# Differential attention on one core: GpSimd combines the two attention maps by itself, and the transposes follow two steps behind

## The chip, the cores and the metric

The kernel runs on one core of a Trainium2 chip. The metric is the device time of one execution in microseconds (us), as the median of several runs.

## The reference, cut to what matters

One layer of a hybrid backbone works on 2048 sample tokens and 128 prompt tokens. It normalises and projects them, runs a differential attention beside a short gated convolution, and projects the result. The change touches the attention of the sample tokens alone:

```python
s = einsum('bqhmd,bkhmd->bhmqk', qblk, k) * scale     # m = 0, 1: two maps per head
p = softmax(s, axis=-1)
a = p[:, :, 0] - lam * p[:, :, 1]                     # the combine
out = einsum('bhqk,bkhe->bqhe', a, v)
```

There are 4 heads, 2048 queries and 2176 keys (2048 samples and 128 cached ones), head dimension 64 and value dimension 128. All is float32.

## The kernel before, in words

The kernel has five stages: modulation, projections, convolution, attention (about 935 us to 1718 us of the profiled execution) and the output projection. Each engine has a program of its own, written out by hand; engines meet only at semaphores (`wait_ge`), and each engine takes its instructions in order.

**Attention** goes in 64 steps (NT), one for each head and tile of 128 queries. Step n works on the scores of tile n and on later stages of earlier tiles. It has four parts, p = 0 to 3. In each part TensorE (PE) computes 128x1024 scores of one map and one half of the keys (L761), VectorE (DVE) takes their maximum (L1380), and ScalarE (ACT) writes their exponentials to `e0` (map 0, four buffers) or `e1` (map 1, two buffers) with the sums beside them (L1070). The 128 cached keys are a small third piece (`PIECES`: 0 to 1024, 1024 to 2048, 2048 to 2176). Scores alternate between two pairs of PSUM banks, so part p waits for the exponentials of part p - 2.

Each piece has a maximum of its own. So small operations bring the pieces to one scale: DVE L1402 and L1405 at the end of step n, an exponential on ACT (L1082), then in part 0 of step n + 1 DVE L1388, L1394 and L1398 (the reciprocal of the softmax sum). GpSimd (POOL) waits for L1398 and makes six factors per row from it (L596, L598): one for each map and piece, with 1 or -lambda in it.

**The combine** of tile n, before the change, is divided. GpSimd multiplies all three pieces of `e1` by their factors (L603, with the factor broadcast as a second tensor), then the middle piece of `e0` (L606), and adds the two middle pieces (L610). VectorE does the first and the third piece in one pass each (`combine`, L1362: `e0` times factor plus `e1`), two steps behind the scores (S_COMB = 2), in part 0 and part 2.

**Behind it**, three steps behind (S_TR = 3), PE transposes the 17 blocks of the combined map (L742, groups of 4, 4, 4, 4 and 1). ACT copies the groups 0, 1, 2 and 4 out of PSUM (L1023), and DVE copies group 3 (`tr_dve`, L1355). Group 3 shares its bank with group 1 of the next tile, so PE waits for that copy (L738). Five steps behind (S_PV = 5), the product with v is made for two tiles at once, a half of the keys in each step (L750), and ACT takes it out (L1031) and stores it (S_OUT = 7).

The order of DVE's work in part 0 is: maximum, combine of piece 0, L1388, `tr_dve`, L1394, L1398. SP loads q for each step, k once per head, and v in two halves when the products of the last head have released them.

After step 63 come drain steps. In them DVE also splits blocks of `w_out` (`wo_lo`, L1347) and does the softmax of the prompt (`prompt_maps`). ACT waits for blocks of `w_out`, and SP loads the next ones when DVE has released their buffer. The output stage begins with a PE operation at L819.

Of the kernel before, what the change touches and what calls it, by code (L numbers as in the profile page):

```python
# [61 lines left out]
S_COMB, S_TR, S_PV, S_OUT = 2, 3, 5, 7  # L62
# [12 lines left out]
def hymba_layer(nc, a):  # L75
# [8 lines left out]
    with ctx:  # L84
# [25 lines left out]
        tick = sb("tick", [P, 1])  # L110
        cw = sb("cw", [P, 4])
# [199 lines left out]
        def _(sp):  # L311
# [157 lines left out]
            for it in range(ITS):  # L469
                head = it // 4  # L470
                for t in range(4):
                    sp.wait_ge(s_pair, 4 * (4 * it + t + 1))
                    if it == 4 * (H - 1) and t == 0:
                        load_wo(0)
                        load_wo(1)
                    if it % 4 == 0 and t == 0 and head + 1 < H:
                        load_k(head + 1)
                    if it % 4 == 0 and head > 0 and t == 3:
                        sp.wait_ge(pv_mm, 4 * it - 1)
                        load_v(head, 0)  # L480
                    if it % 4 == 1 and head > 0 and t == 0:
                        sp.wait_ge(pv_mm, 4 * (it - 1))
                        load_v(head, 1)
                    if it + 1 < ITS:
                        load_q(t, (it + 1) // 4, ((it + 1) % 4) * 4 * P + t * P)
# [60 lines left out]
        def _(pool):  # L546
# [73 lines left out]
        def _(pe):  # L620
# [109 lines left out]
            def transposes(n, t, g):  # L730

                j0, cnt = TGROUPS[g]
                if g == 0:
                    pe.wait_ge(a_ready, 2 * (n + 1))
                    pe.wait_ge(a1_ready, n + 1)

                if g == 1:
                    wait(pe, t_dve, n)  # L738
                else:
                    wait(pe, t_act, {0: 4 * n - 1, 2: 4 * n + 1, 3: 4 * n + 2, 4: 4 * n}[g])  # L740
                for i in range(cnt):
                    mm = pe.transpose(trbank(g)[:, i * P:(i + 1) * P], e0[:, t, (j0 + i) * P:(j0 + i + 1) * P], ident)  # L742
                mm.then_inc(t_mm, 1)
# [20 lines left out]
            def step(it, t, sc=True, tr=True, tr_last=True, pv=True):  # L764
                n = 4 * it + t
                for p in range(4):
# [12 lines left out]
                    if pv:  # L779
                        half = 1 - t % 2  # L780
                        b = 0 if t in (1, 2) else 1
                        if p == 1 - half:
                            pe.wait_ge(s_v[half], (32 if half else 16) * ((it + (2 if t == 0 else 3)) // 4))
                            if half == 0:
                                pe.wait_ge(t_act, 4 * (n - 4) + 3)
                                wait(pe, att_evac, 2 * it - (2 if t == 1 else 1))
                            else:
                                pe.wait_ge(t_act, 4 * (n - 4))
                                pe.wait_ge(t_dve, n - 4)
                        product(b, half, p)  # L790
# [17 lines left out]
            for n in range(NT, NT + S_PV):  # L808
                step(n // 4, n % 4, sc=False, tr=n < NT + S_TR, tr_last=n <= NT + S_TR)
                if n == NT + 2:  # L810
                    prompt_transposes()
                if n == NT + 4:
                    prompt_product()
# [41 lines left out]
        def _(act):  # L855
# [170 lines left out]
            def att_out(it, t):  # L1026

                pb = 1 if t == 1 else 0
                act.wait_ge(pv_mm, 4 * it + t - S_PV)
                wait(act, att_stored[pb], 16 * (it - (2 if t == 1 else 1)))  # L1030
                act.activation(atto[:, pb], ps[:, 7, pb * 2 * P:(pb + 1) * 2 * P], ACT.Copy).then_inc(att_evac, 1)  # L1031

            def att_store(it, t):

                pb = 1 if t == 1 else 0
                act.wait_ge(att_evac, 2 * it - (2 if t == 1 else 1))
                u = it - (2 if t == 1 else 1)
# [7 lines left out]
            def step(it, t, sc=True, tr=True, tr_last=True, out=True):  # L1045
                n = 4 * it + t
                b = t % 2
                for p in range(4):
# [3 lines left out]
                    if sc and p == 3:  # L1052
                        act.wait_ge(mxc_done, n + 1)
                        wait(act, a_ready, 2 * (n - 1))
# [6 lines left out]
                    if sc:  # L1061
# [3 lines left out]
                        if p == 2:  # L1065
                            wait(act, a_ready, 2 * (n - 1) - 1)
                        if p == 3:
                            wait(act, a1_ready, n - 1)
# [15 lines left out]
            for it in range(3):  # L1084
                for t in range(4):
                    n = 4 * it + t
                    step(it, t, tr=n >= S_TR, tr_last=n > S_TR, out=n >= S_OUT and t % 2 == 1)
            with act.Fori(3, ITS) as it:
                for t in range(4):
                    step(it, t, out=t % 2 == 1)  # L1090
            for n in range(NT, NT + S_OUT - 1):
                step(n // 4, n % 4, sc=False, tr=n < NT + S_TR, tr_last=n <= NT + S_TR,
                     out=n % 2 == 1)
# [4 lines left out]
                if n == NT + 2:  # L1098
                    act.wait_ge(a_ready, 2 * NT)
# [46 lines left out]
        def _(dve):  # L1146
# [224 lines left out]
            def step(it, t, sc=True, den=True, comb=True, tr_last=True):  # L1371
                n = 4 * it + t
                b = t % 2
                for p in range(4):
# [9 lines left out]
                    if p == 0 and comb:  # L1384
                        combine(n - S_COMB, (t - S_COMB) % 4, 0)
# [4 lines left out]
                    if p == 0 and tr_last:  # L1390
                        tr_dve(n - 1 - S_TR, (t - 1 - S_TR) % 4)
# [15 lines left out]
                    if p == 2 and comb:  # L1407
                        combine(n - S_COMB, (t - S_COMB) % 4, 2)
# [5 lines left out]
            for it in range(2):  # L1414
                for t in range(4):
                    n = 4 * it + t
                    step(it, t, den=n >= 1, comb=n >= S_COMB, tr_last=n > S_TR)
# [3 lines left out]
            for n in range(NT, NT + S_TR + 1):  # L1421
                step(n // 4, n % 4, sc=False, den=n == NT, comb=n < NT + S_COMB, tr_last=n <= NT + S_TR)
# [136 lines left out]
```

## Time and profile before

| | us |
|---|---|
| median of 3 runs | 1938.04 (1937.11 to 1943.31) |
| the profiled execution | 1940.76 |
| its span in the profile | 1939.0 |
| PE busy (8596 instructions) | 1763.6 (91%) |
| DVE busy (1500) | 1173.9 (61%) |
| POOL busy (614) | 749.1 (39%) |
| ACT busy (1505) | 720.2 (37%) |
| mean granted TensorE clock | 0.971 of full speed |

A row of the timeline gives the start, the duration, the engine, the line, the operation and what it writes and reads; in square brackets stands how long the engine was idle before it and what released it. Rows of one line that follow each other closely are merged (x3). Times are us, in groups also ns where marked. PE's ends are modelled. PEld is the loading of PE's weights.

### The profile page before, as it was taken

What the parts mean: (1) busy time and instruction counts of PE and PEld (TensorE: products, weight loads), DVE (VectorE), ACT (ScalarE), POOL (GpSimd) and SP (SyncE); (2) the same over time, 40 slices, a digit from 0 to 9 for tenths busy, and PEclk for the clock granted to TensorE, in tenths of its full rate; (3) what the DMA queues carried; (4) which work ended last, traced back from release to release, by engine and by line L of the source; (5) the groups of instructions that cost most, each with busy time, mean ns of one, the idle gap of its engine ahead of it and who ended that gap; (6) DMA issues with size and microseconds to landing.
All of it is one profiled execution on the core that took longest, in us unless ns stands there. A gap on an engine that the chain in (4) does not pass through costs nothing.

```text
span 1939.0 us, 25390 instructions
## 1 busy us (share of the span) xinstructions
PE 1763.6 (91%) x8596; PEld 1488.4 (77%) x8596; DVE 1173.9 (61%) x1500; ACT 720.2 (37%) x1505; POOL 749.1 (39%) x614
## 2 busy tenths in 40 slices
PE   7799999989999999998589999889999999659999
PEld 2478888878999989998367777767777777548889
DVE  0554588872232332423688888888888888655553
ACT  2443233331010100100466666666666666431110
POOL 0000488880000000000477777777777777400000
PEclk9899999999999999999799999999999999879999
DMA  9233222331020110101710031113001100146441
GB/s 352 95 109 104 80 99 91 105 117 52 29 90 19 41 68 28 68 19 45 186 35 29 27 85 39 31 47 79 27 27 51 53 27 16 46 170 241 176 141 48
DMA packets 121890, 154.79 MB, mean 80 GB/s; under 512 B 10224, under 2 KB 111344, under 8 KB 120688
## 3 DMA queue, kind: packets, MB, share of 16 engines
q1 hardware_dynamic: 116704, 149.69, 24.0%
q10 hardware_dynamic: 5136, 4.46, 0.7%
q8 instruction: 28, 0.46, 0.1%
q14 instruction: 22, 0.18, 0.0%
HBM read 104.04 MB, written 50.07 MB: 79 GB/s over the span
## 4 chain that ended last, share of the span: by engine, by line
PE 68%; DVE 16%; issue 6%; DMA 4%; ACT 3%; SPq 2%; POOL 0%; DVEq 0%; ACTq 0%; POOLq 0%
PE ps L634 34%; PE ps L836 10%; PE ps L761 8%; DVE e L1362 8%; PE ps L750 7%; PE ps L742 4%; PE ps L626 3%; DVE stt L1380 2%; ACT scr L919 2%; PE ps L651 2%; DVE at L1355 1%; DMA wad<-in_w_ada 1%; PE ps L819 1%; DMA worw<-in_w_out 1%; ACT scr L881 1%
## 5 line engine op out<-in xcount | busy, mean ns | idle before, releaser
L634 PE MATMUL ps<-hT,w 128*128 128x448 f32 (+1 forms) x3360 | 694.1, 366 | 12.6 <-DVE w L1169 12.6
L634 PEld LDWEIGHTS ps<-hT,w 128*128 128x128 f32 x3360 | 623.9, 189 | 76.2 <-issue 27.1
L761 PE MATMUL ps<-kb,qb 128*128 (+1 forms) x1280 | 340.0, 397 | 47.9 <-ACT e L1070 30.8
L1070 ACT ACTIVATE e<-ps,stt 128x1024 f32<-128x1024 f32 x256 | 285.7, 1116 | 259.3 <-DVE stt L1380 235.7
L1380 DVE TENSOR_REDUCE stt<-ps 128x1 f32<-128x1024 f32 x256 | 312.2, 1220 | 97.3 <-PE ps L761 96.9
L750 PE MATMUL ps<-at,vb 128*128 128x256 f32 x1088 | 281.2, 390 | 9.2 <-ACT atto L1031 9.2
L761 PEld LDWEIGHTS ps<-kb,qb 128*128 128x128 f32 x1280 | 208.1, 194 | 84.3 <-ACT e L1070 39.3
L596 POOL TENSOR_TENSOR stt<-stt,lamc 128x2 f32<-128x2 f32 x64 | 12.6, 197 | 660.9 <-DVE stt L1398 660.9
L603 POOL TENSOR_TENSOR e<-e,stt 128x1024 f32<-128x1024 f32 (+1 forms) x192 | 262.8, 1397 | 5.0
L750 PEld LDWEIGHTS ps<-at,vb 128*128 128x128 f32 x1088 | 211.1, 197 | 48.4 <-issue 9.7
L742 PE MATMUL ps<-cst,e 128*128 128x128 f32 x1088 | 175.7, 280 | 57.6 <-DVE at L1355 56.6
L1362 DVE SCALAR_TENSOR_TENSOR e<-e,stt 128x1024 f32<-128x1024 f32 (+1 forms) x128 | 225.6, 1762 | 0.0
L742 PEld LDWEIGHTS ps<-cst,e 128*128 128x128 f32 x1088 | 131.0, 142 | 112.0 <-DVE at L1355 82.1
L836 PE MATMUL ps<-mix,wo 128*128 128x448 f32 (+1 forms) x960 | 205.1, 373 | 7.2 <-DVE mix L1455 7.2
L836 PEld LDWEIGHTS ps<-mix,wo 128*128 128x128 f32 x960 | 181.7, 192 | 27.5 <-DVE mix L1455 7.6
L610 POOL TENSOR_TENSOR e<-e 128x1024 f32<-128x1024 f32 x64 | 152.5, 2383 | 9.2
L985 ACT ACTIVATE scr<-ps 128x448 f32<-128x448 f32 (+1 forms) x40 | 20.9, 533 | 352.7 <-PE ps L634 352.7
L1217 DVE RECIPROCAL qx<-qx 128x448 f32<-128x448 f32 (+1 forms) x40 | 114.8, 2870 | 49.8 <-ACT qx L950 49.7
L565 POOL TENSOR_TENSOR qx<-qx,scr 128x448 f32<-128x448 f32 (+1 forms) x40 | 45.8, 1146 | 241.3 <-DVE qx L1221 238.9
L1023 ACT ACTIVATE at<-ps 128x512 f32<-128x512 f32 (+1 forms) x256 | 124.3, 511 | 23.1 <-PE ps L742 22.8
L606 POOL TENSOR_TENSOR e<-e,stt 128x1024 f32<-128x1024 f32 x64 | 125.2, 1956 | 0.0
L634 PE MATMUL ps<-w,hT 128*128 128x512 f32 x408 | 98.1, 401 | 7.3 <-DVE hT L1201 7.3
(108 smaller groups left out, 1374.4 us busy)
## 6 DMA issues: line engine op xcount, KB each, us to landing
raw<-in_w_in SPq DMA_DIRECT2D x32, 512.0 KB, 3.8
qb<-spill_q SPq DMA_DIRECT2D x256, 64.0 KB, 2.3
wad<-in_w_ada SPq DMA_DIRECT2D x6, 2048.0 KB, 9.0
scr<-in_xT SPq DMA_DIRECT2D x8, 1024.0 KB, 5.7
kb<-spill_k SPq DMA_DIRECT2D x8, 1024.0 KB, 9.7
spill_k<-scr SPq DMA_DIRECT2D x32, 224.0 KB, 2.1
spill_q<-scr SPq DMA_DIRECT2D x32, 224.0 KB, 2.2
spill_cv<-scr SPq DMA_DIRECT2D x32, 224.0 KB, 2.2
```

The costliest lines, as they stand in the source:

```text
L603: pool.tensor_tensor(e1[:, b, k0:k1], e1[:, b, k0:k1], stt[:, b, 7, 3 + c:4 + c].to_broadcast([P, k1 - k0]), ALU.mult)\
L606: pool.tensor_tensor(e0[:, t, k0:k1], e0[:, t, k0:k1], stt[:, b, 7, 1:2].to_broadcast([P, k1 - k0]), ALU.mult)\
L610: pool.tensor_tensor(e0[:, t, k0:k1], e0[:, t, k0:k1], e1[:, b, k0:k1], ALU.add).then_inc(a1_ready, 1)
L634: mm = pe.matmul(out, slot_of(l, j), rhs_of(r, j), start=(i == 0 and j == 0), stop=(i == 2 and j == DJ - 1))
L742: mm = pe.transpose(trbank(g)[:, i * P:(i + 1) * P], e0[:, t, (j0 + i) * P:(j0 + i + 1) * P], ident)
L750: mm = pe.matmul(ps[:, 7, b * 2 * P:(b + 1) * 2 * P], vb[:, js[i]], at[:, b, 0, js[i], :], start=(half == 0 and i == 0), stop=(half == 1 a ...
L761: mm = pe.matmul(out[:, c0 - k0:c1 - k0], qb[:, t, ver, m], keys, start=(ver == 0), stop=(ver == 1))
L836: mm = pe.matmul(ps[:, k % 4, 0:n], wo[:, o, l, j], mix[:, tg % 2, r, j, 0:n], start=(half == 0 and i == 0 and j == H), stop=(half == 1 an ...
L1023: act.activation(at[:, t // 2, 0, j0:j0 + cnt, (t % 2) * P:(t % 2 + 1) * P], trbank(g).rearrange("p (j q) -> p j q", j=cnt), ACT.Copy).the ...
L1070: act.activation(dst[:, c * 1024:(c + 1) * 1024], ps[:, 2 * c:2 * c + 2, :].rearrange("p c n -> p (c n)"), ACT.Exp, bias=stt[:, b, 0, 3 * ...
L1362: dve.scalar_tensor_tensor(e0[:, t, k0:k1], e0[:, t, k0:k1], stt[:, t % 2, 7, c:c + 1], e1[:, t % 2, k0:k1], ALU.mult, ALU.add).then_inc(a ...
L1380: dve.tensor_reduce(stt[:, b, 0, 3 * m + c:3 * m + c + 1], ps[:, 2 * c:2 * c + 2, :].rearrange("p c n -> p (c n)"), AX.X, ALU.max, negate= ...
```

## The change

GpSimd multiplies both maps, piece by piece, with `tensor_scalar` and the factor as a per-partition scalar. It does so in two parts: the first 1024 keys with their own sum (and the semaphore `a_ready`), then the other 1152 keys (`a1_ready`). One small operation (into a new tile `gate`) stands before the first multiplication. VectorE does nothing of the combine, and copies group 3 before L1388. Transposes, products and stores each come one step earlier; group 0 waits for the first part, group 2 for the second. The halves of the product, the loads of v and the waits are renumbered to match.

```diff
-S_COMB, S_TR, S_PV, S_OUT = 2, 3, 5, 7
+S_TR, S_PV, S_OUT = 2, 4, 6
...
-                    if it % 4 == 0 and head > 0 and t == 3:
+                    if it % 4 == 0 and head > 0 and t == 2:
                         sp.wait_ge(pv_mm, 4 * it - 1)
                         load_v(head, 0)
-                    if it % 4 == 1 and head > 0 and t == 0:
-                        sp.wait_ge(pv_mm, 4 * (it - 1))
+                    if it % 4 == 0 and head > 0 and t == 3:
+                        sp.wait_ge(pv_mm, 4 * it)
                         load_v(head, 1)
...
+            def pieces(n, t, which):
+                b = t % 2
+                for c in which:
+                    k0, k1 = PIECES[c]
+                    pool.tensor_scalar(e1[:, b, k0:k1], e1[:, b, k0:k1], stt[:, b, 7, 3 + c:4 + c], None, ALU.mult)\
+                        .then_inc(e1_done, 1)
+                    pool.tensor_scalar(e0[:, t, k0:k1], e0[:, t, k0:k1], stt[:, b, 7, c:c + 1], None, ALU.mult)\
+                        .then_inc(e0_done, 1)
...
                 pool.wait_ge(coef_done, n + 1)
-                for c in (0, 2, 1):
-                    k0, k1 = PIECES[c]
-                    pool.tensor_tensor(e1[:, b, k0:k1], e1[:, b, k0:k1],
-                                       stt[:, b, 7, 3 + c:4 + c].to_broadcast([P, k1 - k0]), ALU.mult)\
-                        .then_inc(e1_done, 1)
-                pool.tensor_tensor(e0[:, t, k0:k1], e0[:, t, k0:k1], stt[:, b, 7, 1:2].to_broadcast([P, k1 - k0]), ALU.mult)\
-                    .then_inc(e0_done, 1)
+                pool.tensor_tensor(gate[:], lamc[:], lamc[:], ALU.mult)
+                pieces(n, t, (0,))
+                pool.wait_ge(e1_done, 3 * n + 1)
+                pool.wait_ge(e0_done, 3 * n + 1)
+                pool.tensor_tensor(e0[:, t, 0:1024], e0[:, t, 0:1024], e1[:, b, 0:1024], ALU.add).then_inc(a_ready, 1)
+                pieces(n, t, (1, 2))
                 pool.wait_ge(e1_done, 3 * (n + 1))
-                pool.wait_ge(e0_done, n + 1)
-                pool.tensor_tensor(e0[:, t, k0:k1], e0[:, t, k0:k1], e1[:, b, k0:k1], ALU.add).then_inc(a1_ready, 1)
+                pool.wait_ge(e0_done, 3 * (n + 1))
+                pool.tensor_tensor(e0[:, t, 1024:KEYS], e0[:, t, 1024:KEYS], e1[:, b, 1024:KEYS], ALU.add)\
+                    .then_inc(a1_ready, 1)
...
                 if g == 0:
-                    pe.wait_ge(a_ready, 2 * (n + 1))
+                    pe.wait_ge(a_ready, n + 1)
+                if g == 2:
                     pe.wait_ge(a1_ready, n + 1)
...
-            def combine(n, t, c):
-
-                k0, k1 = PIECES[c]
-                dve.wait_ge(e1_done, 3 * n + (1 if c == 0 else 2))
-                dve.scalar_tensor_tensor(e0[:, t, k0:k1], e0[:, t, k0:k1], stt[:, t % 2, 7, c:c + 1],
-                                         e1[:, t % 2, k0:k1], ALU.mult, ALU.add).then_inc(a_ready, 1)
...
-                    if p == 0 and comb:
-                        combine(n - S_COMB, (t - S_COMB) % 4, 0)
+                    if p == 0 and tr_last:
+                        tr_dve(n - 1 - S_TR, (t - 1 - S_TR) % 4)
                     if p == 0 and den:
                         dve.wait_ge(f_done, n)
                         dve.tensor_tensor(stt[:, 1 - b, 4, :], stt[:, 1 - b, 3, :], stt[:, 1 - b, 1, :], ALU.mult)\
                             .then_inc(fz_done, 1)
-                    if p == 0 and tr_last:
-                        tr_dve(n - 1 - S_TR, (t - 1 - S_TR) % 4)
...
-                    if p == 2 and comb:
-                        combine(n - S_COMB, (t - S_COMB) % 4, 2)
```

## Rows read from the trace of the kernel before

**Rows 1.** Busy by stretch: length; PE, PEld, DVE, ACT, POOL; clock, DMA.
```profile
1240.00:1560.00 320.00, 287.73 (x1509) 233.64 (x1510) 273.24 (x365) 208.43 (x487) 244.91 (x196) 0.98 0.16 46
```

**Rows 2.** Who waited for whom, 1000 to 1560 us: total us, times, longest.
```profile
POOL stt L596 <- DVE stt L1398: 119.0, 48, 4.1
...
PEld ps L742 <- DVE at L1355: 60.4, 48, 2.1
```

**Rows 3.** Chain that ended last, 1240 to 1300 us: start us, us, what.
```profile
1260.59 2.25 DVE e L1362
...
1262.91 0.61 DVE at L1355
...
1263.57 0.66 PE ps L742 x4
```

**Rows 4.** Timeline of POOL: one step; first and last L596 of 64.
```profile
941.95 0.20 POOL L596 TENSOR_TENSOR stt<-stt,lamc 128x2 f32<-128x2 f32 x1 [508.41 <-DVE stt L1398]
...
1263.86 0.20 POOL L596 TENSOR_TENSOR stt<-stt,lamc 128x2 f32<-128x2 f32 x1 [2.10 <-DVE stt L1398]
...
1264.42 4.10 POOL L603 TENSOR_TENSOR e<-e,stt 128x1024 f32<-128x1024 f32 x3
1268.48 1.94 POOL L606 TENSOR_TENSOR e<-e,stt 128x1024 f32<-128x1024 f32 x1
1270.57 2.38 POOL L610 TENSOR_TENSOR e<-e 128x1024 f32<-128x1024 f32 x1
...
1666.30 0.23 POOL L596 TENSOR_TENSOR stt<-stt,lamc 128x2 f32<-128x2 f32 x1 [2.10 <-DVE stt L1398]
```

**Rows 5.** Busy by stretch: two neighbouring steps (columns of rows 1).
```profile
1263.86:1275.28 11.42, 11.42 (x64) 9.56 (x63) 9.29 (x14) 7.35 (x17) 8.79 (x8) 1.00 0.08 23
1275.28:1286.45 11.17, 8.79 (x50) 6.92 (x49) 10.28 (x14) 7.63 (x18) 8.77 (x8) 1.00 0.11 35
```

**Rows 6.** Groups by form on POOL: busy us, mean ns of one.
```profile
L603 POOL TENSOR_TENSOR e<-e,stt 128x1024 f32<-128x1024 f32 x128 | 242.5, 1895 | 5.0
L610 POOL TENSOR_TENSOR e<-e 128x1024 f32<-128x1024 f32 x64 | 152.5, 2383 | 9.2
L606 POOL TENSOR_TENSOR e<-e,stt 128x1024 f32<-128x1024 f32 x64 | 125.2, 1956 | 0.0
...
L603 POOL TENSOR_TENSOR e<-e,stt 128x128 f32<-128x128 f32 x64 | 25.7, 402 | 0.0
```

**Rows 7.** Groups by form on ACT and DVE: busy us, mean ns of one.
```profile
L1070 ACT ACTIVATE e<-ps,stt 128x1024 f32<-128x1024 f32 x256 | 285.7, 1116 | 259.3 <-DVE stt L1380 235.7 <-PE ps L742 23.3
...
L1362 DVE SCALAR_TENSOR_TENSOR e<-e,stt 128x1024 f32<-128x1024 f32 x64 | 116.2, 1815 | 0.0
L1362 DVE SCALAR_TENSOR_TENSOR e<-e,stt 128x128 f32<-128x128 f32 x64 | 109.4, 1709 | 0.0
...
L1057 ACT ACTIVATE e<-ps,stt 128x128 f32<-128x128 f32 x128 | 45.9, 364 | 18.9 <-DVE stt L1411 18.9
```

**Rows 8.** Timeline around one held DVE operation, about 1317 us.
```profile
1315.84 2.37 POOL L610 TENSOR_TENSOR e<-e 128x1024 f32<-128x1024 f32 x1
...
1317.17 1.05 DVE L1405 TENSOR_TENSOR stt<-stt 128x6 f32<-128x6 f32 x1
```

**Rows 9.** Timeline of DVE: L1388 before the L596 of rows 4.
```profile
1262.76 0.15 DVE L1388 TENSOR_TENSOR stt<-stt 128x6 f32<-128x6 f32 x1
```

**Rows 10.** Busy by stretch: a lower clock (columns of rows 1).
```profile
1309.00:1323.00 14.00, 14.00 (x70) 11.68 (x70) 10.55 (x15) 7.47 (x17) 9.44 (x10) 0.88 0.52 118
```

**Rows 11.** Timeline of the drain, 1683 to 1718 us.
```profile
1683.17 0.68 DVE L1355 COPY at<-ps 128x512 f32<-128x512 f32 x1
...
1691.33 0.69 DVE L1355 COPY at<-ps 128x512 f32<-128x512 f32 x1 [7.22 <-PE ps L742]
...
1696.93 2.36 DVE L1347 TENSOR_TENSOR wo<-worw,wo 128x1024 fp32r<-128x1024 f32 x2 [4.90 <-ACT wo L1015]
...
1718.19 1.86 PE L819 MATMUL ps<-csq,cst 128*128 128x448 f32 x2 [11.47 <-ACT csq L1118]
```

More of the change, by code:

```diff
@@ L110, in hymba_layer @@
         tick = sb("tick", [P, 1])
+        gate = sb("gate", [P, 2])
         cw = sb("cw", [P, 4])
@@ L779, in step @@
                     if pv:
-                        half = 1 - t % 2
-                        b = 0 if t in (1, 2) else 1
+                        half = t % 2
+                        b = t // 2
                         if p == 1 - half:
-                            pe.wait_ge(s_v[half], (32 if half else 16) * ((it + (2 if t == 0 else 3)) // 4))
+                            pe.wait_ge(s_v[half], (32 if half else 16) * ((it + 3) // 4))
                             if half == 0:
-                                pe.wait_ge(t_act, 4 * (n - 4) + 3)
-                                wait(pe, att_evac, 2 * it - (2 if t == 1 else 1))
-                            else:
-                                pe.wait_ge(t_act, 4 * (n - 4))
-                                pe.wait_ge(t_dve, n - 4)
+                                pe.wait_ge(t_act, 4 * (n - 3) + 3)
+                                wait(pe, att_evac, 2 * it - (2 if t == 0 else 1))
+                            else:
+                                pe.wait_ge(t_act, 4 * (n - 3))
+                                pe.wait_ge(t_dve, n - 3)
                         product(b, half, p)
@@ L811, in _ @@
                     prompt_transposes()
-                if n == NT + 4:
+                if n == NT + 3:
                     prompt_product()
@@ L1026, in att_out @@
             def att_out(it, t):
-                pb = 1 if t == 1 else 0
+                pb = 1 if t == 0 else 0
                 act.wait_ge(pv_mm, 4 * it + t - S_PV)
-                wait(act, att_stored[pb], 16 * (it - (2 if t == 1 else 1)))
+                wait(act, att_stored[pb], 16 * (it - (2 if t == 0 else 1)))
                 act.activation(atto[:, pb], ps[:, 7, pb * 2 * P:(pb + 1) * 2 * P], ACT.Copy).then_inc(att_evac, 1)
             def att_store(it, t):
-                pb = 1 if t == 1 else 0
-                act.wait_ge(att_evac, 2 * it - (2 if t == 1 else 1))
-                u = it - (2 if t == 1 else 1)
+                pb = 1 if t == 0 else 0
+                act.wait_ge(att_evac, 2 * it - (2 if t == 0 else 1))
+                u = it - (2 if t == 0 else 1)
                 q0 = (u % 4) * (4 * P) + pb * 2 * P
@@ L1053, in step @@
                         act.wait_ge(mxc_done, n + 1)
-                        wait(act, a_ready, 2 * (n - 1))
+                        wait(act, a1_ready, n - 1)
                         for mc in range(2):
@@ L1065, in step @@
                         if p == 2:
-                            wait(act, a_ready, 2 * (n - 1) - 1)
-                        if p == 3:
-                            wait(act, a1_ready, n - 1)
+                            wait(act, a_ready, n - 1)
                         dst = e0[:, t] if m == 0 else e1[:, b]
@@ L1086, in _ @@
                     n = 4 * it + t
-                    step(it, t, tr=n >= S_TR, tr_last=n > S_TR, out=n >= S_OUT and t % 2 == 1)
+                    step(it, t, tr=n >= S_TR, tr_last=n > S_TR, out=n >= S_OUT and t % 2 == 0)
             with act.Fori(3, ITS) as it:
                 for t in range(4):
-                    step(it, t, out=t % 2 == 1)
+                    step(it, t, out=t % 2 == 0)
             for n in range(NT, NT + S_OUT - 1):
                 step(n // 4, n % 4, sc=False, tr=n < NT + S_TR, tr_last=n <= NT + S_TR,
-                     out=n % 2 == 1)
+                     out=n % 2 == 0)
                 if n == NT:
@@ L1098, in _ @@
                 if n == NT + 2:
-                    act.wait_ge(a_ready, 2 * NT)
+                    act.wait_ge(a_ready, NT)
                     act.wait_ge(a1_ready, NT)
@@ L1369, in three, with step @@
                 return x.rearrange("p (m c) -> p m c", m=2)
-            def step(it, t, sc=True, den=True, comb=True, tr_last=True):
+            def step(it, t, sc=True, den=True, tr_last=True):
                 n = 4 * it + t
@@ L1416, in _ @@
                     n = 4 * it + t
-                    step(it, t, den=n >= 1, comb=n >= S_COMB, tr_last=n > S_TR)
+                    step(it, t, den=n >= 1, tr_last=n > S_TR)
             with dve.Fori(2, ITS) as it:
@@ L1420, in _ @@
                     step(it, t)
-            for n in range(NT, NT + S_TR + 1):
-                step(n // 4, n % 4, sc=False, den=n == NT, comb=n < NT + S_COMB, tr_last=n <= NT + S_TR)
+            for n in range(NT, NT + S_TR + 2):
+                step(n // 4, n % 4, sc=False, den=n == NT, tr_last=n <= NT + S_TR)
                 if n == NT:
```

## The prediction

> **What bounds the kernel now.** I first read the busy time by stretch, to find the stage that matters and how full each engine is in it. In the attention PE is busy 287.7 of 320 us, DVE 273.2, POOL 244.9 and ACT 208.4 [rows 1]. No engine is full, so the next view is who waits for whom. PE waits for DVE's copy of group 3 (60.4 us in 48 waits of its weight loads), and POOL waits for DVE's reciprocal, 119.0 us in 48 waits [rows 2]. The chain of waits says why: the combine L1362 (2.25 us) stands before the copy, and the transposes start at once behind the copy [rows 3]. So DVE, in order and with 3.5 us of combine in each step (1.815 + 1.709 us), sets the pace [rows 7]. Of that 3.5 us a large part is standing still: the piece of 128 columns takes 1709 ns, almost as long as the one of 1024.
>
> The first L596 is at 941.95 and the last of 64 at 1666.30 [rows 4]. That is 724.35 us for 63 steps, 11.5 us for one. Two neighbouring steps take 11.42 and 11.17 us; PE is busy 11.42 and 8.79 of them, 20.2 us in two [rows 5]. So PE alone would allow 10.1 us a step, and POOL needs 9.1 us from L596 to the end of L610 (1263.86 to 1272.95) [rows 4].
>
> **DVE's part.** 3.5 us a step go. The 320 us of [rows 1] hold 28 steps, with 9.8 us of DVE in each; 6.3 are left. DVE then has room, and the copy of group 3 comes right behind the first maximum. PE's wait for it goes. What is late next is POOL.
>
> **POOL's step, added up.** Now it has six multiplications and two sums. The sums have a row: 2.38 us for 1024 columns [rows 4]; for 1152 columns 2.65 us, with (2383 - 189) / 1024 = 2.14 ns for each column more [rows 6]. The multiplication with a per-partition scalar has none on POOL. Its bounds come from two rows. From above, the multiplication by a broadcast tensor: 1895 ns for 1024 columns and 402 for 128, so 1.67 ns a column and 189 ns fixed [rows 6]. From below, an engine that reads one tensor and takes a per-partition operand: ACT's exponentials take 1116 ns for 1024 columns and 364 for 128, so 0.84 ns a column [rows 7]. The first is 1.99 times the second, as if POOL spent one slot of 0.84 ns on each operand that it reads, even on one number read again and again. With one operand read, one slot is left: 189 + 1024 x 0.84 = 1.05 us, and 0.30 us for 128 columns. I take that, because the operands are ACT's kind and the fixed part is POOL's. The ends are 0.9 us (ACT's slot, hardly any fixed part) and 1.9 us.
>
> Consecutive POOL instructions start 0.04 us before the last one's end (4.10 us for three that last 4.19), and a sum waits 0.15 us behind the product that it needs [rows 4]. The step then runs: L596 at 0, the small operation into the gate tile at 0.56 (where the first product is now), the first product at 0.72, the second at 1.73, the sum at 2.93. The other four products start at 5.26, 6.27, 7.28 and 7.54, the second sum at 7.99, and it ends at 10.64. That is 10.6 us, more than PE's 10.1: POOL becomes the bound. To it I add 0.1 for two DVE operations that slip in between (L606, with a held one behind it, takes 1956 ns against 1895 [rows 6]) and 0.2 for reading six scalars, a guess whose ends are 0 and 0.6. **10.9 us a step.**
>
> Because POOL is the bound from its first tile on (steps 0 and 1 have no transposes), it needs no wait for DVE: 63 x 10.9 = 686.7 us against 724.35, **37.7 us less**. Now and then a step takes about 1.9 us more while the granted clock is lower, 0.88 in such a stretch [rows 10]. POOL's backlog covers these; if that cover were gone, seven of them would give back 13 us.
>
> **Waits.** Group 0 wants the first part, ready 5.3 us after L596, and group 2 the second, at 10.7. PE reaches group 2 of tile n half way through step n + 2, some 14 us behind L596 of tile n. So a POOL step of up to 11 us is in time, and what PE waits is POOL's pace, not latency. ACT's third part of step n waits for the first part of tile n - 2, which is long done. The four buffers of `e0` suffice, since the transposes come earlier too. SP's loads of v move one step up with the products that release and need them; the distance is the same, and the load of q behind them is wanted a whole round later. I cost these at nothing; a load of v that came late would be seen once per head. The small operation is counted above (0.16 us).
>
> **The drain.** From the last L596 to the first L819 it is 51.9 us (1666.30 to 1718.19) [rows 4, 11]. Behind the prompt's softmax DVE copies a group 3 at 1683.17 and the next at 1691.33, and only at 1696.93 come the third and fourth block of w_out, on which loads and the output stage hang [rows 11]. With S_TR = 2 one tile fewer is open there: 1683.17 to 1691.33, **8.2 us less**. The ends are 0 (the loads of w_out set it anyway) and 13.8 (1683.17 to 1696.93, all of it).
>
> **Sum.** -37.7 - 8.2 = -45.9 us: the profiled execution's 1940.8 (span 1939.0 and 1.8 around it) becomes 1894.9. The median of the runs is 2.7 us below that execution, so 1892 us. A difference under 0.3% (6 us) can't be told from none.
>
> **Rivals.**
> *A. POOL's product stays slow.* One operand less does not help, because the loop over columns sets the time. At the broadcast row's 1.9 us the step is 10.9 + 4 x 0.84 + 2 x 0.1 = 14.5 us, so 63 x 14.5 = 913 us, and 1938 + 189 - 8 = 2119 us. It is slower from (724.35 + 8.2) / 63 = 11.6 us a step, a product of 1.22 us. For it: every large POOL row here is at 1.67 ns a column or above. Against it: the factor of 1.99. I give 0.12 to about 1.9 us and 0.11 to values between 1.25 and 1.7 us (1941 to 2062 us). The Trainium skill, GPSIMD Engine Reference, section on elementwise work, gives about 1.8 cycles an element as the best case of a tight loop; an estimate from that is 1.7 us a product and 13.6 us a step, which is in this case. The same page calls one-input work roughly line rate, which is in mine; no row here decides between them.
>
> *B. DVE and POOL lock each other out (slower).* A DVE operation of six columns, L1405, takes 1.05 us at 1317.17 and ends when POOL's sum ends (1315.84 + 2.37 = 1318.21) [rows 8]. L1388 is of the same kind, and it starts 1.1 us before the L596 that depends on it [rows 4, 9]. Before, POOL is always idle at that moment. Now it is in its last sum for 2.65 us. If L1388 arrives there, it is held to the end, and 1.1 us pass before POOL goes on: 10.8 + 1.1 = 11.9 us a step, 750 us, 1938 + 25 - 8 = 1955 us. It decides if L1388 comes later than 8.0 us into POOL's step. Against it: POOL starts with a backlog, as steps 0 and 1 are short, and PE's own wait for group 2 places L1388 at about 7.3 us. That is close; a step at the lower clock may tip it. Chance 0.12. The Trainium skill, SBUF — State Buffer, "Who interferes with whom", says that a VectorE instruction with two SBUF inputs and a reading GpSimd instruction exclude each other for a whole instruction; by that rule the trace agrees, with the 1.05 us above.
>
> *C. POOL is faster than I take it.* At 0.9 us a product and no time for scalars the step is 10.1 us, where PE is the bound: 636 us, 1938 - 88 - 8 = 1842 us at best, 1867 with half way to it. Chance 0.07.
>
> *D. About nothing.* A product of 1.2 us and 11.6 us a step: chance 0.06.
>
> **How the numbers follow.** My case (products of 1.0 to 1.15 us) has 0.52: 1875 to 1920 us. The range from 1866 to 1968 takes in this, D, B and about half of C and the near end of A's middle values; it leaves out the slow product and most of its middle. Faster is my case, C and a little of D: 0.60. Same is the rest of D: 0.05. Slower is A and B: 0.35.
>
> **What the profile after would show.** POOL busy for over 9 of 11 us, with hardly any idle time before L596; a product of about 1.05 us for 1024 columns; 63 steps in about 687 us. No combine on DVE, no wait of PE for L1355, instead one for POOL at group 2. L1388 and L1405 at times held for up to 2.6 us. What would make me wrong: a product over 1.22 us, or idle time of 1.1 us before L596 in each step while L1388 lasts over 1 us (rival B), or PE full again.

## The result, and the profile after

The changed kernel takes 2367.09 us (median of 4 runs, 2364.85 to 2370.27), the kernel before 1937.57 beside it: a ratio of 1.221, with a 95% interval from 1.218 to 1.224. It is slower by 430 us. The prediction was 1892 us, with a range up to 1968; even its slowest rival ended at 2119.

GpSimd's groups by form in the changed kernel (busy us, mean ns of one; the rows of before are [rows 6]):

```profile
L601 POOL TENSOR_SCALAR e<-e,stt 128x1024 f32<-128x1024 f32 x128 | 365.4, 2855 | 0.0
L599 POOL TENSOR_SCALAR e<-e,stt 128x1024 f32<-128x1024 f32 x128 | 364.3, 2846 | 0.1
L620 POOL TENSOR_TENSOR e<-e 128x1152 f32<-128x1152 f32 x64 | 167.0, 2609 | 9.5
L616 POOL TENSOR_TENSOR e<-e 128x1024 f32<-128x1024 f32 x64 | 150.1, 2346 | 9.5
...
L601 POOL TENSOR_SCALAR e<-e,stt 128x128 f32<-128x128 f32 x64 | 38.7, 605 | 0.0
L599 POOL TENSOR_SCALAR e<-e,stt 128x128 f32<-128x128 f32 x64 | 38.7, 604 | 0.0
```

The product with a per-partition scalar takes 2.85 us for 1024 columns and 0.60 for 128. I had put it at 1.05 and 0.30, with 1.9 as the upper end for 1024. The two sums are as computed (2.35 and 2.61 us against 2.38 and 2.65). One step of GpSimd, with the start of the next, and the first and last of the 64 (timeline; [rows 4] before):

```profile
939.11 0.20 POOL L607 TENSOR_TENSOR stt<-stt,lamc 128x2 f32<-128x2 f32 x1 [503.80 <-DVE stt L1399]
...
1509.94 0.20 POOL L607 TENSOR_TENSOR stt<-stt,lamc 128x2 f32<-128x2 f32 x1
1510.21 0.20 POOL L609 TENSOR_TENSOR stt<-stt 128x6 f32<-128x6 f32 x1
1510.49 0.20 POOL L612 TENSOR_TENSOR gate<-lamc 128x2 f32<-128x2 f32 x1
1510.66 2.85 POOL L599 TENSOR_SCALAR e<-e,stt 128x1024 f32<-128x1024 f32 x1
1513.49 2.85 POOL L601 TENSOR_SCALAR e<-e,stt 128x1024 f32<-128x1024 f32 x1
1516.48 2.37 POOL L616 TENSOR_TENSOR e<-e 128x1024 f32<-128x1024 f32 x1
...
1525.81 2.61 POOL L620 TENSOR_TENSOR e<-e 128x1152 f32<-128x1152 f32 x1
1528.37 0.20 POOL L607 TENSOR_TENSOR stt<-stt,lamc 128x2 f32<-128x2 f32 x1
...
2099.11 0.20 POOL L607 TENSOR_TENSOR stt<-stt,lamc 128x2 f32<-128x2 f32 x1
```

Only the first L607 has idle time before it: from then on GpSimd never waits for VectorE, and a step is what its instructions add up to, 18.4 us (1509.94 to 1528.37). The 63 steps take 1160.0 us against 724.35, so +435.7. The drain, from the last L607 to the first operation of the output stage (2145.89), is 46.8 us against 51.9, so -5.1; the first combine starts 2.8 us earlier. That sums to +427.8 us, beside 426.5 by the spans (2365.5 and 1939.0).

The same stretch as [rows 1] (columns as there), and the waits in 1000 to 1560 us (us in total, times, longest; [rows 2] before):

```profile
1240.00:1560.00 320.00, 218.20 (x951) 174.75 (x950) 132.24 (x193) 132.62 (x304) 312.15 (x191) 0.85 0.11 30
```

```profile
DVE stt L1383 <- PE ps L773: 321.1, 122, 7.0
...
PE ps L754 <- POOL e L620: 99.4, 30, 4.4
...
PE ps L754 <- POOL e L616: 77.6, 30, 5.0
```

GpSimd is busy for 312 of 320 us; PE fell from 288 to 218, and waits for both sums (L616, L620). No wait for DVE's copy is left. The granted clock is 0.85 in this stretch, against 0.98. PE's idle time goes before the low clock in these rows (busy by stretch, columns of [rows 1]):

```profile
1506.20:1510.10 3.90, 0.00 (x0) 0.00 (x0) 0.00 (x0) 0.78 (x2) 3.75 (x4) 0.89 0.00 0
1510.10:1511.20 1.10, 1.09 (x5) 1.10 (x6) 0.00 (x0) 0.00 (x0) 0.94 (x4) 0.50 0.00 0
...
1516.30:1518.90 2.60, 2.31 (x13) 1.63 (x11) 1.23 (x2) 0.00 (x0) 2.45 (x3) 1.00 1.02 202
```

PE does nothing for 3.9 us, then works at 0.50, the lower of its two levels (1.2 of 2.4 GHz), where four transposes take 1.11 us, and later at 1.00, where they take 0.60. The same comes again a step later, at 1528.50 us. Since GpSimd's chain has no gaps, the low clock costs the steps nothing.

### The profile page after: what moved, and what is told of

It reads as the page before. It is cut to its first block, busy times and chain, and to the rows that moved or that the text cites. A ratio compares the mean times of both kernels' runs of the same rounds, so it can differ in the third digit from the quotient of the medians.

```text
span 2365.5 us, 25394 instructions
## 1 busy us (share of the span) xinstructions
PE 1899.8 (80%) x8596; PEld 1595.3 (67%) x8596; DVE 1033.2 (44%) x1372; ACT 727.2 (31%) x1505; POOL 1336.1 (56%) x870
## 4 chain that ended last, share of the span: by engine, by line
POOL 42%; PE 40%; issue 9%; DMA 3%; DVE 3%; ACT 2%; SPq 0%; POOLq 0%; ACTq 0%; DVEq 0%
PE ps L645 28%; POOL e L601 17%; POOL e L599 17%; PE ps L848 8%; POOL e L620 5%; PE ps L637 2%; ACT scr L931 1%; PE ps L662 1%; DMA wad<-in_w_ada 1%; POOL e L616 1%; PE ps L831 1%; DMA worw<-in_w_out 1%; POOL stt L609 1%; POOL gate L612 1%; DMA raw<-in_w_in 1%
## 5 line engine op out<-in xcount | busy, mean ns | idle before, releaser
L754 PE MATMUL ps<-cst,e 128*128 128x128 f32 x1088 | 220.9, 330 | 381.3 <-POOL e L620 213.1
L754 PEld LDWEIGHTS ps<-cst,e 128*128 128x128 f32 x1088 | 159.5, 170 | 457.4 <-issue 160.2
L773 PE MATMUL ps<-kb,qb 128*128 (+1 forms) x1280 | 406.6, 457 | 20.0 <-DMA kb<-spill_k 16.1
L601 POOL TENSOR_SCALAR e<-e,stt 128x1024 f32<-128x1024 f32 (+1 forms) x192 | 404.1, 2105 | 0.0
L599 POOL TENSOR_SCALAR e<-e,stt 128x1024 f32<-128x1024 f32 (+1 forms) x192 | 403.0, 2099 | 0.1
L762 PE MATMUL ps<-at,vb 128*128 128x256 f32 x1088 | 328.8, 440 | 0.0
L607 POOL TENSOR_TENSOR stt<-stt,lamc 128x2 f32<-128x2 f32 x64 | 12.6, 197 | 503.8 <-DVE stt L1399 503.8
L773 PEld LDWEIGHTS ps<-kb,qb 128*128 128x128 f32 x1280 | 251.5, 232 | 54.5 <-issue 19.1
L762 PEld LDWEIGHTS ps<-at,vb 128*128 128x128 f32 x1088 | 246.6, 230 | 53.6
L1035 ACT ACTIVATE at<-ps 128x512 f32<-128x512 f32 (+1 forms) x256 | 130.9, 513 | 289.6 <-PE ps L754 289.5
L620 POOL TENSOR_TENSOR e<-e 128x1152 f32<-128x1152 f32 x64 | 167.0, 2609 | 9.5
L616 POOL TENSOR_TENSOR e<-e 128x1024 f32<-128x1024 f32 x64 | 150.1, 2346 | 9.5
```

The lines of the kernel that those rows point to most:

```text
L599: pool.tensor_scalar(e1[:, b, k0:k1], e1[:, b, k0:k1], stt[:, b, 7, 3 + c:4 + c], None, ALU.mult)\
L601: pool.tensor_scalar(e0[:, t, k0:k1], e0[:, t, k0:k1], stt[:, b, 7, c:c + 1], None, ALU.mult)\
L616: pool.tensor_tensor(e0[:, t, 0:1024], e0[:, t, 0:1024], e1[:, b, 0:1024], ALU.add).then_inc(a_ready, 1)
L620: pool.tensor_tensor(e0[:, t, 1024:KEYS], e0[:, t, 1024:KEYS], e1[:, b, 1024:KEYS], ALU.add)\
L762: mm = pe.matmul(ps[:, 7, b * 2 * P:(b + 1) * 2 * P], vb[:, js[i]], at[:, b, 0, js[i], :], start=(half == 0 and i == 0), stop=(half == 1 a ...
L773: mm = pe.matmul(out[:, c0 - k0:c1 - k0], qb[:, t, ver, m], keys, start=(ver == 0), stop=(ver == 1))
```

## The experiments

Theory 1 was that GpSimd is the only bound and that the price of its single-operation product, above what the broadcast product costs, explains the time. Its rival, theory 2, was that the new structure (two parts, two steps behind, small VectorE operations among long GpSimd ones) costs something by itself. Each ratio is to the kernel before, run beside it on the same chip; its median was 1940.6 to 1941.1 us.

**1. The broadcast product back**

```diff
-pool.tensor_scalar(e1[:, b, k0:k1], e1[:, b, k0:k1], stt[:, b, 7, 3 + c:4 + c], None, ALU.mult)
+pool.tensor_tensor(e1[:, b, k0:k1], e1[:, b, k0:k1],
+                   stt[:, b, 7, 3 + c:4 + c].to_broadcast([P, k1 - k0]), ALU.mult)   # and e0 likewise
```

> The changed kernel, but GpSimd multiplies with tensor_tensor and the factor broadcast, as the kernel before did; all else as changed. Theory 1 (GpSimd is the only bound, and its product with a per-partition scalar, 2.85 us for 1024 columns and 0.60 for 128, is the whole loss): a step is 18.4 us less 4 x 0.97 and 2 x 0.22, so 14.1 us, and the run takes 2367 - 63 x 4.3 = 2095 us. Theory 2 (the two-part structure or the distance of two steps costs something by itself, by waits and held VectorE operations): it stays above 2150 us, with idle time on GpSimd.

Measured: 2095.7 us, ratio 1.080 (1.078 to 1.081). Steps run from 942.92 to 1830.63, so 14.09 us each, with no idle time before L609 (L607 of the changed kernel) but before the first. Theory 1 holds to a microsecond; 271 of the 430 us are the choice of this instruction. The other 155 us or so are what the moved work costs even at the broadcast product's 1.90 us, where PE would allow 10.1 us a step. The structure itself costs nothing that shows at this pace.

**2. A price list.** Ahead of the first combine, GpSimd does single operations on spare tiles, each waited for:

```diff
+for i in range(3): done(pool.tensor_scalar(v[:, 0:1024], v[:, 0:1024], s, None, ALU.mult))              # L639
+for i in range(3): done(pool.tensor_scalar(v[:, 0:512], v[:, 0:512], s, None, ALU.mult))                # L641
+for i in range(3): done(pool.tensor_scalar(v[:, 0:1024], v[:, 0:1024], 0.5, None, ALU.mult))            # L643
+...
+for i in range(3): done(pool.tensor_scalar(v[:, 0:1024], v[:, 0:1024], s, 0.5, ALU.mult, ALU.add))      # L647
+for i in range(3): done(pool.tensor_copy(v[:, 0:1024], w_[:, 0:1024]))                                  # L649
+...
```

> The changed kernel, with 29 GpSimd operations more ahead of the first combine, one after the other, on spare tiles: products with a per-partition scalar, with a constant, with a scalar and a second constant, copies, products with a broadcast and with a full tensor. Theory 1a (reading the scalar through a pointer is what costs): with a constant the product of 1024 columns takes about 1.05 us, and with a pointer 2.85. Theory 1b (the loop of this operation costs it, whatever the scalar is): both take 2.85 us, and the copy, which reads one tensor too, says whether one read is cheap at all (1.05 us) or not. The total says nothing; it is that of the changed kernel and some 50 us.

The whole run, one execution, took 2416.5 us; its rows by form (mean ns of one) are what counts:

```profile
L639 POOL TENSOR_SCALAR vpad<-vpad,sublns 128x1024 f32<-128x1024 f32 x3 | 8.5, 2848 | 0.3
L643 POOL TENSOR_SCALAR vpad<-vpad 128x1024 f32<-128x1024 f32 x3 | 8.3, 2770 | 0.3
...
L653 POOL TENSOR_TENSOR vpad<-vpad,sublns 128x1024 f32<-128x1024 f32 x3 | 5.7, 1893 | 0.2
L641 POOL TENSOR_SCALAR vpad<-vpad,sublns 128x512 f32<-128x512 f32 x3 | 4.7, 1564 | 0.3
L647 POOL TENSOR_SCALAR vpad<-vpad,sublns 128x1024 f32<-128x1024 f32 x3 | 3.4, 1122 | 0.3
L649 POOL COPY vpad<-ppad 128x1024 f32<-128x1024 f32 x3 | 3.1, 1040 | 0.2
...
L651 POOL COPY vpad<-ppad 128x128 f32<-128x128 f32 x3 | 0.9, 296 | 0.2
```

The pointer is not to blame: with a constant the product still takes 2.77 us, so theory 1a falls. One more column costs this form (2848 - 1564) / 512 = 2.51 ns, and the copy (1040 - 296) / 896 = 0.83 ns. But the same instruction with a second operation (times the scalar, plus a constant) takes 1.12 us, hardly more than a copy. Neither theory had that.

**3. Products as short as the prediction took them to be.** They run over 306 and 6 columns; the kernel leaves the other columns without their factor.

```diff
+cut = k0 + (306 if c < 2 else 6)
-pool.tensor_scalar(e1[:, b, k0:k1], e1[:, b, k0:k1], stt[:, b, 7, 3 + c:4 + c], None, ALU.mult)
+pool.tensor_scalar(e1[:, b, k0:cut], e1[:, b, k0:cut], stt[:, b, 7, 3 + c:4 + c], None, ALU.mult)   # and e0 likewise
```

> The changed kernel with products over 306 of each 1024 columns and 6 of 128, so that each takes the 1.05 and 0.30 us that the prediction had assumed (the other columns are left without their factor). Theory 1 (only the price of the product was wrong): a step takes 10.6 to 10.9 us, 63 steps 668 to 687 us, and the run 1875 to 1900 us, as predicted for that price (1892). Theory 2 (VectorE's small operations and GpSimd lock each other out, or the new structure waits): 11.9 us a step and 1955 us or more, with 1.1 us of idle time before each L607.

Measured: 1884.9 us, ratio 0.971 (0.969 to 0.972). The products take 1.07 us, 63 steps run from 941.40 to 1621.83, so 10.80 us each, and the drain is 42.5 us. At the price that I had assumed, the total of the prediction (1892 us) was right to 0.4%, and its parts, 10.9 and 43.7 us, to 1% and 3%. The lockout of rival B does happen in small: L1407, six columns wide, takes 1.7 us on average.

```profile
L1407 DVE TENSOR_TENSOR stt<-stt 128x6 f32<-128x6 f32 x64 | 110.1, 1721 | 2.2
...
L1392 DVE TENSOR_TENSOR stt<-stt 128x6 f32<-128x6 f32 x64 | 14.7, 229 | 0.0
```

But it is L1407 (L1405 before) that is held, at the end of a step, and hardly L1392 (L1388 before), on which GpSimd waits: 0.23 us against 0.15. So the loop does not close.

**4. VectorE's order alone, in the kernel before**

```diff
-if p == 0 and comb: combine(n - S_COMB, (t - S_COMB) % 4, 0)
+if p == 0 and tr_last: tr_dve(...)            # now directly behind the maximum
 ...                                           # L1388
-if p == 0 and tr_last: tr_dve(...)
 ...                                           # L1394 and L1398, now L1392 and L1396
+if p == 0 and comb: combine(n - S_COMB, (t - S_COMB) % 4, 0)
```

> The kernel before, with one thing moved in VectorE's part 0: the copy of group 3 directly behind the maximum, and the combine of piece 0 last, behind the reciprocal. Nothing is taken from GpSimd or VectorE. Theory 3 (the kernel before was held up by the order on VectorE, not by the amount of its work): the wait of the transposes for the copy (1.7 us in every second step) goes, a step takes 10.9 to 11.1 us instead of 11.5, and the run 1900 to 1912 us. Rival (the combine only moves its delay onto the next maximum): 1932 to 1944 us.

Measured: 1882.6 us, ratio 0.970 (0.969 to 0.971), a step of 10.62 us (941.90 to 1610.75). That is below the range of the theory (10.9 to 11.1 us, 1900 to 1912 us). The waits from 1000 to 1560 us show what went; first the kernel before, then this run:

```profile
PE ps L742 <- DVE at L1355: 40.7, 24, 1.7
...
PE ps L742 <- DVE at L1355: 8.4, 27, 0.3
```

PE's wait for the copy is nearly gone, and GpSimd waits 26.2 us for the reciprocal, against 119.0. The theory had left out one part of the gain: in the kernel before, eight of the 63 steps take 13.0 to 13.2 us, the others 11.27 on average. Here one takes 12.06 us and no other more than 10.66, and the granted clock from 1240 to 1560 us is 1.00 instead of 0.98. So of the 55.5 us that 63 steps gain, some 14 are the long steps and some 41 the rest.

The groups show what became of the held operations (mean ns; [rows 7] before):

```profile
L1362 DVE SCALAR_TENSOR_TENSOR e<-e,stt 128x1024 f32<-128x1024 f32 x64 | 82.1, 1282 | 0.0
L1405 DVE TENSOR_TENSOR stt<-stt 128x6 f32<-128x6 f32 x64 | 79.3, 1238 | 2.2
...
L1388 DVE TENSOR_TENSOR stt<-stt 128x6 f32<-128x6 f32 x64 | 45.2, 706 | 0.0
...
L1362 DVE SCALAR_TENSOR_TENSOR e<-e,stt 128x128 f32<-128x128 f32 x64 | 28.1, 439 | 0.0
```

Last in part 0 the combine starts just before GpSimd's step (at 1260.33 us, L596 at 1260.47) and is not held: 1282 instead of 1815 ns. The small piece, whose place in part 2 is the same, falls from 1709 to 439. Most of that moved to L1405 (1238 instead of 308) and L1388 (706 instead of 154): the four together take 3.67 us a step instead of 3.99. So the gain is not less holding in sum; other operations are held, and PE's transposes no longer wait behind the combine. The kernel before was bound by the order on VectorE, not by the amount of its work, and moving the combine to another engine was not needed for this gain. The edit moves the copy forward and the combine back at once; which of the two counts for more was not tried.

**5. The changed kernel with two-operation products**

```diff
-pool.tensor_scalar(..., stt[:, b, 7, 3 + c:4 + c], None, ALU.mult)
+pool.tensor_scalar(..., stt[:, b, 7, 3 + c:4 + c], 0.0, ALU.mult, ALU.add)      # and e0 likewise
```

> The changed kernel, with a second operation in each product: times the per-partition scalar, plus the constant 0. In the price list a product with a scalar and a second constant took 1.12 us for 1024 columns, the one without 2.85. Theory 1 (the single-operation form is what costs, and GpSimd is the bound): the step of the short products, 10.80 us with 1.07 us each, becomes 11.05 us, 63 steps 696 us, the run 1885 + 16 = 1901 us. Rival (the low price holds only alone, and beside VectorE's work or on two maps in turn it does not): products above 2 us and a run above 2100 us.

Measured: 1906.8 us, ratio 0.983 (0.981 to 0.985), 11.12 us a step (937.74 to 1638.10), as theory 1 said but for 6 us. The timeline of a step:

```profile
1250.39 1.12 POOL L599 TENSOR_SCALAR e<-e,stt 128x1024 f32<-128x1024 f32 x1
1251.48 1.12 POOL L601 TENSOR_SCALAR e<-e,stt 128x1024 f32<-128x1024 f32 x1
1252.75 2.36 POOL L616 TENSOR_TENSOR e<-e 128x1024 f32<-128x1024 f32 x1
...
1257.29 0.36 POOL L599 TENSOR_SCALAR e<-e,stt 128x128 f32<-128x128 f32 x1
```

One more operation in the instruction, on the same data, makes the kernel 460 us faster than the changed one. It is then 34 us faster than the kernel before, but GpSimd is still the bound (no idle time before L607 but before the first), and it loses to experiment 4.

**6. Order and two-operation products together, on the kernel before** (the edits of 4 and 5 on GpSimd's four products, with the gate operation ahead)

> The kernel before with VectorE's order of e4_order_in_before, and GpSimd's four products by the two-operation form (with the small operation into the gate tile ahead of them). GpSimd's work falls from 9.1 to about 6.9 us a step, and VectorE's held operations wait for shorter ones. Theory 3 (PE, at 10.1 us a step, is nearly the bound in e4, where a step takes 10.6): 10.2 to 10.4 us a step, 1855 to 1870 us. Rival (what is left between 10.6 and 10.1 is latency between PE, VectorE and ScalarE, not holding): 1878 to 1887 us, as e4.

Measured: 1875.3 us, ratio 0.967 (0.965 to 0.968), 10.46 us a step (939.25 to 1598.31). That is in neither range, between the two: 2 us less work on GpSimd gave 0.16 us a step. The gain on experiment 4 is 7 us, or 0.4%. The intervals lie edge to edge (from 0.9685 in 4, up to 0.9684 in 6), so it is small and only just clear of noise. The held operations did not become shorter in sum, and GpSimd is held in turn, as in experiment 4: L597, two columns wide, takes 1.2 us, and ends with VectorE's combine (1253.18 + 1.28).

```profile
1253.18 1.28 DVE L1363 SCALAR_TENSOR_TENSOR e<-e,stt 128x1024 f32<-128x1024 f32 x1
...
1253.32 1.20 POOL L597 TENSOR_TENSOR stt<-stt,lamc 128x2 f32<-128x2 f32 x1 [2.30 <-DVE stt L1397]
```

**7. A second price list** (each line three times, each operation waited for)

```diff
+tensor_scalar(v[:, 0:1024], v[:, 0:1024], s, 0.0, ALU.mult, ALU.add)      # L639
+tensor_scalar(v[:, 0:1024], v[:, 0:1024], s, 1.0, ALU.mult, ALU.mult)     # L641
+tensor_scalar(v[:, 0:1024], v[:, 0:1024], s, s, ALU.mult, ALU.mult)       # L643
+tensor_scalar(v[:, 0:1024], v[:, 0:1024], 0.5, 0.5, ALU.mult, ALU.add)    # L645
+tensor_scalar(v[:, 0:1024], v[:, 0:1024], s, None, ALU.add)               # L647
+tensor_scalar(v[:, 0:1024], w_[:, 0:1024], s, None, ALU.mult)             # L649
+...
+tensor_scalar(v[:, 0:128], v[:, 0:128], s, 0.0, ALU.mult, ALU.add)        # L653
```

> A second price list ahead of the first combine, all with 1024 columns where not said: scalar and 0 (times, plus), scalar and 1 (times, times), scalar twice (times, times), two constants, scalar alone with plus in place of times, scalar alone with another output tile, and the two-operation form with 512 and 128 columns. Theory 1c (any form with two operations runs in a fast loop of 0.84 ns a column, any with one in a slow loop): 1.12 us for the first four, 2.8 us for the single plus and the single one into another tile. Theory 1d (only times with plus is fast): times, times takes 2 us or more. The total says nothing.

The whole run, one execution, took 2413.1 us. The rows:

```profile
L649 POOL TENSOR_SCALAR vpad<-ppad,sublns 128x1024 f32<-128x1024 f32 x3 | 8.5, 2846 | 0.3
L647 POOL TENSOR_SCALAR vpad<-vpad,sublns 128x1024 f32<-128x1024 f32 x3 | 8.5, 2844 | 0.3
...
L643 POOL TENSOR_SCALAR vpad<-vpad,sublns 128x1024 f32<-128x1024 f32 x3 | 3.6, 1193 | 0.3
L639 POOL TENSOR_SCALAR vpad<-vpad,sublns 128x1024 f32<-128x1024 f32 x3 | 3.4, 1126 | 0.3
L641 POOL TENSOR_SCALAR vpad<-vpad,sublns 128x1024 f32<-128x1024 f32 x3 | 3.4, 1122 | 0.3
L645 POOL TENSOR_SCALAR vpad<-vpad 128x1024 f32<-128x1024 f32 x3 | 3.1, 1047 | 0.3
...
L653 POOL TENSOR_SCALAR vpad<-vpad,sublns 128x128 f32<-128x128 f32 x3 | 1.1, 373 | 0.3
```

Theory 1c holds for all that was tried, on float32: the four forms with two operations (times and plus, times and times, with constants or pointers) are fast, the forms with one slow, times or plus, in place or into another tile. One more column costs the fast form (1126 - 373) / 896 = 0.84 ns, the same as ACT's exponential, on which the prediction had bet.

**8. Two-operation products alone, in the kernel before**

```diff
-pool.tensor_tensor(e1[...], e1[...], stt[:, b, 7, 3 + c:4 + c].to_broadcast([P, k1 - k0]), ALU.mult)
+pool.tensor_scalar(e1[...], e1[...], stt[:, b, 7, 3 + c:4 + c], 0.0, ALU.mult, ALU.add)     # and e0 likewise
```

> The kernel before with its own order on VectorE; only GpSimd's four products are changed to the two-operation form (with the small operation into the gate tile). GpSimd has 2 us of idle time in each step before, so by busy time nothing could come of this: 1935 to 1944 us. Theory 4 (VectorE's combine is held until GpSimd's running operation ends: 1.7 us for 128 columns that take 0.33 alone, and 1.8 for 1024 that take 1.2): holding ends after 1.1 us instead of 1.9, a step takes 0.5 to 1 us less, and the run 1878 to 1910 us.

Measured: 1915.0 us, ratio 0.987 (0.985 to 0.989), 11.07 us a step (942.96 to 1640.29). That is outside both ranges, 5 us above that of theory 4 (1878 to 1910 us) and 20 us below that of its rival. The direction is that of theory 4, and the size smaller than it said. GpSimd waits for the reciprocal in each step (210.9 us in 50 waits, from 1000 to 1560 us), and yet its shorter instructions are worth 26 us. The groups fit the reason given:

```profile
L1363 DVE SCALAR_TENSOR_TENSOR e<-e,stt 128x1024 f32<-128x1024 f32 x64 | 81.4, 1272 | 0.0
L1406 DVE TENSOR_TENSOR stt<-stt 128x6 f32<-128x6 f32 x64 | 60.6, 947 | 2.2
...
L1363 DVE SCALAR_TENSOR_TENSOR e<-e,stt 128x128 f32<-128x128 f32 x64 | 34.5, 539 | 0.0
```

With L1389 (0.15 us as before) the four take 2.91 us a step instead of 3.99. PE's wait for the copy stays (43.2 us in 25 waits), and so do long steps (nine of 13.1 us): the part that the order on VectorE costs.

**9. Three steps behind again**

```diff
-S_TR, S_PV, S_OUT = 2, 4, 6
+S_TR, S_PV, S_OUT = 3, 5, 7      # with the halves, loads and waits of the kernel before; all else as in 5
```

> The changed kernel with the two-operation products (e5), but transposes, products and stores three, five and seven steps behind, as in the kernel before: the distance alone is undone. Theory (the distance is worth one tile in the drain and nothing in the steps, GpSimd being the bound): a step stays at 11.1 us, the stretch from the last combine's start to the output stage grows from 42.7 to 50 to 52 us, and the run is 1907 + 8 = 1915 us. Rival (nearer transposes also save waits in the steps): a step of 11.3 us or more, and 1925 us or above.

Measured: 1911.4 us, ratio 0.985 (0.983 to 0.987), 11.10 us a step, 45.7 us of drain against 42.7 in experiment 5. The pace does not depend on the distance, GpSimd being the bound. The drain was expected at 50 to 52 us: the nearer transposes are worth some 3 us there, not 8, and the intervals of 5 and 9 overlap.

**10. A version that divides the work by columns**

```diff
-pool.tensor_scalar(e0[:, t, k0:k1], ...)                 # second part, two-operation form
+pool.tensor_scalar(e0[:, t, k0:kz], ...)                 # kz = 1536 for the middle piece
-pool.tensor_tensor(e0[:, t, 1024:KEYS], ..., ALU.add)
+pool.tensor_tensor(e0[:, t, 1024:1536], ..., ALU.add); pool.tensor_tensor(e0[:, t, SAMPLE:KEYS], ..., ALU.add)
+dve.scalar_tensor_tensor(e0[:, (t - 2) % 4, 1536:SAMPLE], ..., stt[:, t % 2, 7, 1:2],
+                         e1[:, t % 2, 1536:SAMPLE], ALU.mult, ALU.add)   # last in part 0, own semaphore
```

> A version that should beat both kernels: e5, but VectorE combines the columns 1536 to 2048 in one pass of 512 columns, last in its part 0, two steps behind, and GpSimd's work on them (half a product and half a sum) goes; transposes stay two steps behind, group 3 waits for VectorE's piece. GpSimd's step falls from 11.1 to about 9.8 us, below PE's 10.1. Theory (PE is the bound then, and the shorter drain is kept): 10.2 to 10.4 us a step, a drain of 43 us, 1852 to 1868 us. Rival (two engines that hold each other again cost as much as in e6_order_and_two_op, 10.46 us a step): 1868 to 1880 us.

Measured: 1857.1 us, ratio 0.956 (0.954 to 0.958), 10.31 us a step (944.41 to 1593.83), 42.4 us of drain. The theory holds for the step, the drain and the total. The stretch from 1240 to 1560 us shows PE nearly full, with GpSimd just below:

```profile
1240.00:1560.00 320.00, 313.71 (x1687) 260.11 (x1686) 250.79 (x376) 224.82 (x551) 304.72 (x375) 1.00 0.18 49
```

## Why the prediction was wrong

**The step that failed** is one term: "With one operand read, one slot is left: 189 + 1024 x 0.84 = 1.05 us". It measured 2.85 us, and 0.60 instead of 0.30 for 128 columns. Four large and two small products add 4 x 1.8 + 2 x 0.3 = 7.8 us to the 10.6 us of the sum, which gives the 18.4 us measured. The 0.3 us that I had added for held operations and the reading of scalars do not show: no run has a row for them, and in experiment 3 the sum with the measured products is 10.74 us, against 10.80. The bounds failed too. The broadcast product was taken as an upper end because it reads more; but price followed the form of the instruction, not the number of operands, and nothing in the trace of before excluded more. A bound has to come from a row of the same form; where there is none, the far end is open, and a term that enters six times should have widened the range beyond rival A's 2119 us.

**The form of the argument misled.** The factor of 1.99 between the broadcast product and ACT's exponential, which I read as two slots against one, fits two more forms: the copy takes 0.83 and the two-operation product 0.84 ns a column, as ACT does. It does not fit the sum of two full tensors (2.14 ns a column, 2.5 slots), which was on record before, nor the single-operation product (2.51 ns, three slots for one tensor read). So counting slots was a guess from two rows. The Trainium skill (GPSIMD Engine Reference, Engine selection) says that one-input work on GpSimd runs at roughly line rate; by that rule the runs agree for the copy (1.04 us) and the two-operation form (1.12 us), and disagree for the single-operation form (2.85 us). The best case of about 1.8 cycles an element in the Trainium skill (GPSIMD Engine Reference, Elementwise), by an estimate at its 1.2 GHz 1.5 ns a column, fits neither form: they take 0.84 and 2.51 ns.

**What was right:** that GpSimd becomes the bound from its first tile, without a wait for VectorE (no idle time before L607), so that 63 steps are 63 times its sum; the sum itself, shown by experiment 3 (10.80 us against 10.9) and 1 (14.09 against the 14.5 of rival A for products of 1.9 us); that a step of 11.6 us breaks even, as far as experiments 5 (11.12, faster) and 1 (14.09, slower) show; that PE's wait for the copy of group 3 goes; and that loads and waits of the shift cost nothing that shows. The drain was right in direction and partly by luck. It is 5.1 us shorter instead of 8.2 here, and 9.4 and 9.2 in experiments 3 and 5. But the reason given, one open tile fewer, is worth only some 3 us (experiments 5 and 9). The other 6 us are there with the old distance too (45.7 us in experiment 9 against 51.9), and come with some other part of the new structure; which one was not tried.

**The rivals.** A had the right mechanism (the loop over columns sets the time) with too small a price. B, the lockout, did not set a pace in any run: VectorE's small operations are held, for up to 2.3 us in the changed kernel, and the pace stays that of GpSimd's own sum. C and D did not occur.

**What I had not asked** is whether the bound of before needed another engine at all. The chain of waits named the combine and its place ahead of the copy; experiment 4 changes the order alone and gains 3%.

Left open: why GpSimd has a slow loop for one operation; and what the small gate operation is for, which was not tried without.

## What to carry to other kernels

Before work moves to an engine, price the very instruction form there, by a few copies of it on spare tiles; a neighbour's price, even on the same engine, is no bound. When an in-order engine bounds a loop, first try to reorder it, so that what others wait for comes first and what nobody waits for comes last. And GpSimd's instruction length matters even when GpSimd has idle time (26 us in experiment 8). In these runs it is the VectorE operations that read two tensors in SBUF that are held: the combine takes up to 3.4 us in the kernel before, and L1391 (L1388 before), 0.15 us alone, up to 2.3 us in the changed one. Those that read one tensor there (L1398 and L1402 before, L1399 and L1403 after) take 166 and 159 ns on average in both kernels.

## What the runs showed of the hardware that I had not expected

- GpSimd's `tensor_scalar` on float32 takes 2.51 ns a column with one operation and 0.84 with two: 2848 against 1126 ns for 128x1024 (experiments 2 and 7). Times the scalar, plus 0, is thus 2.5 times as fast as times the scalar alone; it also beats the broadcast product (1893 ns).
- Holding goes both ways: L597 on GpSimd takes 0.2 us in experiment 8, and 1.2 us in experiment 6, where VectorE's combine of 1.28 us runs beside it.
- Less work for an engine with idle time (experiment 8) and another order at the same work (experiment 4) were worth 26 and 58 us. In this stage, how the engines' instructions meet counted for more than their busy shares.
